# Attention heads on ScalarE: the exponential of a head issued ahead of the copy of the head before it

## What is computed

```
def attend_block(args):                      # a block of 128 query rows
    qb, iqb, iwb, start = args
    tpos = start + jnp.arange(QBLK)
    idx = indexer_topk(iqb, iwb, ik, tpos, k_sel)
    return sparse_attend(qb, k[bi, idx], v[bi, idx], idx, tpos, rel_bias)

def sparse_attend(q, kg, vg, idx, tpos, rel_bias):
    ...
    logits = jnp.einsum('bqhd,bqkhd->bqhk', q, kg).astype(jnp.float32) * (DH_A ** -0.5) + bias
    logits = jnp.where((dist >= 0)[:, :, None, :], logits, -jnp.inf)
    p = jax.nn.softmax(logits, axis=-1).astype(vg.dtype)
    return jnp.einsum('bqhk,bqkhd->bqhd', p, vg)
```

## Time and profile before

| what | value |
|---|---|
| median of 3 executions | 3505.79 us |
| lowest and highest | 3501.47 and 3506.33 us |
| the profiled execution | 3506.33 us |
| its span in the profile | 3504.8 us |
| PE busy in the span | 3318.3 us, 95% |
| DVE, ACT, POOL busy | 1562.3, 1138.2, 1204.6 us |
| mean granted TensorE clock | 0.966 of full speed |

### The profile page before, as it was taken

One profiled execution on the slowest core, in us unless ns is written; L12 is line 12 of the kernel. 1 busy time (PEld: TensorE's weight loads), 2 busy tenths in 40 slices (PEclk: granted clock), 3 DMA queues, 4 the chain that ended last, 5 costly groups with the idle time before them and its releaser, 6 DMA issues. The chain is left out here.

```text
span 3504.8 us, 57096 instructions
## 1 busy us (share of the span) xinstructions
PE 3318.3 (95%) x20476; PEld 3101.8 (89%) x20476; DVE 1562.3 (45%) x2739; ACT 1138.2 (32%) x2092; POOL 1204.6 (34%) x881
## 2 busy tenths in 40 slices
PE   6979989989999999999999999999889999999998
PEld 5569973666999999999899998988789999999998
DVE  4699982542321212122457677667742222212122
ACT  3512212442241312122345545455532322222132
POOL 2206842220412221222445556565444321222122
PEclk8989989996999999999999999999899999999999
DMA  4217654221311111112223232212422111111111
GB/s 130 55 31 135 196 175 137 61 78 50 62 48 48 44 46 48 48 42 65 79 63 98 92 97 78 91 57 91 146 89 89 43 48 48 48 42 48 48 43 72
DMA packets 344005, 263.87 MB, mean 75 GB/s; under 512 B 52134, under 2 KB 308150, under 8 KB 341910
## 3 DMA queue, kind: packets, MB, share of 16 engines
q1 hardware_dynamic: 322726, 232.16, 22.5%
q0 software_dynamic: 8192, 19.13, 1.6%
q10 hardware_dynamic: 12976, 11.11, 1.5%
HBM read 219.43 MB, written 44.76 MB: 75 GB/s over the span
## 5 line engine op out<-in xcount | busy, mean ns | idle before, releaser
L234 POOL TENSOR_TENSOR w_low_sb<-w_loaded_sb,w_high_sb 128x1024 fp32r<-128x1024 f32 (+1 forms) x278 | 570.0, 2057 | 1554.1 <-ACT w_high_sb L226 1536.2
L252 PE MATMUL psum<-act_high_sb,w_high_sb 128*128 128x344 f32 (+1 forms) x2400 | 769.9, 321 | 16.9 <-PEq L2713 10.5
L252 PE MATMUL psum<-act_low_sb,w_high_sb 128*128 128x344 f32 (+1 forms) x2400 | 768.1, 320 | 0.0
L252 PE MATMUL psum<-act_high_sb,w_low_sb 128*128 128x344 f32 (+1 forms) x2400 | 768.0, 320 | 0.0
L252 PE MATMUL psum<-second_high_sb,w_high_sb 128*128 128x344 f32 x1728 | 553.3, 320 | 0.5 <-PEq L2305 0.5
L252 PE MATMUL psum<-second_low_sb,w_high_sb 128*128 128x344 f32 x1728 | 551.9, 319 | 0.0
L252 PE MATMUL psum<-second_high_sb,w_low_sb 128*128 128x344 f32 x1728 | 551.9, 319 | 0.0
L252 PEld LDWEIGHTS psum<-act_high_sb,w_high_sb 128*128 128x128 f32 (+1 forms) x2400 | 451.0, 188 | 17.8 <-issue 16.6
L252 PEld LDWEIGHTS psum<-act_high_sb,w_low_sb 128*128 128x128 f32 (+1 forms) x2400 | 451.3, 188 | 0.4
L252 PEld LDWEIGHTS psum<-act_low_sb,w_high_sb 128*128 128x128 f32 (+1 forms) x2400 | 451.1, 188 | 0.4
L226 ACT CAST w_high_sb<-w_loaded_sb 128x1024 fp32r<-128x1024 f32 (+1 forms) x230 | 239.6, 1043 | 522.1 <-PE psum L252 498.0
(11 more groups left out here) (439 smaller groups left out, 4913.3 us busy)
## 6 DMA issues: line engine op xcount, KB each, us to landing
w_loaded_sb<-in_w_up SPq DMA_DIRECT2D x64, 512.0 KB, 4.1
w_loaded_sb<-in_w_down SPq DMA_DIRECT2D x64, 512.0 KB, 4.2
w_loaded_sb<-in_w_in_odd SPq DMA_DIRECT2D x48, 512.0 KB, 4.0
key_pages_sb<-in_cache_k SPq DMA_DIRECT2D x64, 256.0 KB, 2.8
ecay_sum_spread_sb<-decay_sum_scratch SPq DMA_DIRECT2D x8, 2048.0 KB, 9.8
w_loaded_sb<-in_w_in_even SPq DMA_DIRECT2D x28, 512.0 KB, 4.1
gated_scratch<-gated_sb POOLq DMA_DIRECT2D x8, 1032.0 KB, 4.4
ample_ssm_state_sb<-in_state_ssm SPq DMA_DIRECT2D x64, 128.0 KB, 6.9
```

The lines of the kernel that those rows point to most:

```text
L234: ins = self.nc.gpsimd.tensor_tensor(self.wl[:, par, k, 0:width], self.wf[:, par, k, 0:width], self.wh[:, par, k, 0:width].bitcast(F32), A ...
L252: ins = nc.tensor.matmul(out, w[:, par, k, 0:width], a[:, k, cols], start=n == 0, stop=n == 3 * KT - 1)
```

## The change

ACT's loop over the steps is reordered: in step n the exponential of n is issued first and the copy of the transposed probabilities of n - 1 after it. Before, the copy came first. The waits of each instruction stay with it; every other engine's stream is as it was. The last copy, of step 63, stays behind the loop.

```
             for n in range(N):
                 i, h = seq[n]
                 L = width(i)
-                if n >= 1:
-                    copy_turned(n - 1)
                 act.wait_ge(s_max, n + 1)
                 if h == 0 and i >= 2:
                     act.wait_ge(s_rden, i - 1)
                 nc.scalar.activation(logit[:, n % 2, 0:L], logit[:, n % 2, 0:L], ACT.Exp, bias=nm[:, n % 2:n % 2 + 1],
                                      accum_out=total[:, i % 2, h:h + 1]).then_inc(s_prob, 1)
+                if n >= 1:
+                    copy_turned(n - 1)
                 smp.values_act(act, n)
                 if n >= HA and n % HA == 2:
                     high(n // HA - 1)
```

## The result

The change makes the kernel slower: 3523.88 us as the median of five executions (3521.19 to 3528.72) against 3504.42 for five of before (3501.47 to 3506.33). The ratio is 1.0055 with a 95% interval of 1.0043 to 1.0068. The direction is the forecast one. The size is not: 19.5 us where 9.6 were worked out, and outside the range, whose upper end was 3523. The profiled execution took 3522.86 us. It lies 16.5 us above the profiled execution of before, so 3.0 of the 19.5 us are outside what the two traces can explain.

What follows compares the result with a forecast made beforehand. PE was taken to bound the kernel, busy 95% of the span, so only its gaps count. Terms 3.56 + 3.12 + 1.64 + 1.40 + 0.37 - 0.51 = +9.6 us on 3505.8 gave 3515.4 us, range 3510 to 3523.

Steps and rivals of the forecast that it cites:

- heads 0 to 30: Attention heads where PE's work on the samples' value pages hides the longer chain: cost nothing, upper end +1 us in all.
- head 31: Head whose max waits for VectorE's work on the samples' last values: its transposes come +0.37 us later.
- The odd intervals: Intervals between two heads' transposes that hold score products: no PE gap, to stay at 4.68 us in the last block.
- block 7: Last eight heads: even heads 56, 58, 60, 62 each +0.89 us as the copy waits behind the exponential, 3.56 us.
- block 6: Eight heads before the last block: four even heads at +0.78 us each, 3.12 us.
- block 5: Sixth block of eight heads, max late from VectorE's rotary work: four even heads at 0.41 us, 1.64 us.
- block 4: Fifth block of eight heads: two even heads at the full clock (36, 38) at +0.70 us, 1.40 us.
- last head: Head 63, whose transposes waited for its exponential: that wait goes, -0.51 us.
- Two lags of the chain: Within an even head's chain: copy 0.03 us after the exponential's accumulator, transposes 0.05 us after the copy.
- the clock as a rival: Longer PE idle from block 7's even intervals brings one to three half-clock falls, 3518 to 3530 us; chance 13%.
- all of it PE idle: Profile sign: the 101.4 us stretch, T(35) to the end of weighting, grows by about 9 us, only in PE idle.
- new stretches at clock 0.50: Sign named as showing the prediction wrong: half-clock stretches in the profile that were not there before.

Runs made afterwards that it cites:

- e5: The kernel before with the exponential ahead of the copy in heads 0 to 31 only: 3503.04 us against 3501.00, ratio 1.0006.
- e1: The changed kernel plus eight unused identity transposes on PE ahead of each even head's transposes from 34 on: 3512.64 us against 3503.49 for before, ratio 1.0029.
- e7: The kernel before plus four unused identity transposes on PE ahead of each even head's transposes from 34 on: 3505.25 us against 3501.00, ratio 1.0009.
- e10: The kernel before, each odd head's copy from 35 on done twice, plus eight unused transposes per even head from 34 on: 3512.73 us, ratio 1.0032 to before.
- e8: The changed kernel plus four unused identity transposes on PE ahead of each even head's transposes from 34 on: 3510.75 us against 3501.00 for before, ratio 1.0029.
- e3: The kernel before with the exponential ahead of the copy at even heads only: 3522.95 us, ratio 1.0059 to before.
- e9: The kernel before, its order kept, with the copy of each odd head from 35 on done twice: 3533.92 us against 3501.70, ratio 1.0090.
- e4: The changed kernel with products of heads n+2 and n+3 issued behind the transposes of even n: 3511.13 us against 3503.49 for before, ratio 1.0021.
- e11: As e4, but only from head 36 on; heads 42, 44, 50, 52, 58 keep the old places of products and copy: 3497.86 us against 3501.70, ratio 0.9992.

## Why the prediction was half of it

**Right: what bounds the stage, and which heads pay.** The even heads of blocks 4 to 7 carry the cost, heads 0 to 30 none (0.00 us from head 3 to head 30, in the changed kernel and in e5), head 31 +0.32 us against +0.37, and the next stage takes the shift one for one. The odd intervals stay at PE's own work.

**Right, a little too large: the terms of the order.** From e1, where the clock stays up: block 7 3.27 us (3.56 predicted), block 6 2.83 (3.12), block 5 1.84 (1.64), block 4 1.33 (1.40), last head -0.70 (-0.51). With -0.4 spread over the odd intervals that is the 8.2 us measured, against 3.56 + 3.12 + 1.64 + 1.40 - 0.51 = 9.2. Of the 1.0 us between them, 0.45 lie in the even heads, 0.36 in the odd intervals, which were put at nothing, and 0.19 in the last head. Two lags of the chain were wrong and nearly cancel, which is luck: I let the copy start 0.03 us after the exponential's accumulator had been read, and it starts 0.09 us before that ends (767.08 against 766.98 + 0.19 = 767.17); and I let T(62) start 0.05 us after the copy, where it starts 0.14 after (767.08 + 0.99 = 768.07 to 768.21). Block 5 is luck too. Its term of 0.41 a head was the middle between two arguments, and the heads 40, 42, 44 and 46 measure 0.67, 0.13, 0.33 and 0.71: the full term at two of them and little at the others.

**Wrong: the clock as a rival instead of a term.** The prediction worked out the idle time of 1.40 us in 4.22, saw that PE's busy share there would be lower than in the stretch ahead of the fall at 645.4, and still gave it 13 in 100 with the argument that the gaps so far had been harmless. The step that failed is "Against it: the gaps are split over work that kept the full clock up to now with 0.5 to 0.9 us of idle": a row about small gaps was used for gaps about twice as large, and the sum held nothing for the clock. What the runs show, as the waits of PE ahead of the transposes of the even heads 36 to 62 and the time at half clock in the stretch:

| kernel | waits, us | at half clock, us |
|---|---|---|
| before | 0.07 to 0.92 | 0 |
| e7, before with filler | 0 to 0.47 | 0 |
| e10, doubled copies with filler | 0 to 0.68 | 0 |
| e1, changed with filler | 0 to 0.71 | 0 |
| e8, changed with half the filler | 0.38 to 1.15 | 0 |
| changed | 0.49 to 1.59 | 20.5 |
| e3, exponential first at even heads | 0.06 to 1.59 | 29.1 |
| e9, doubled copies | 0.91 to 1.56 | 37.5 |

In the changed kernel the four falls come 0.4 to 1.6 us after the start of the transposes of heads 36, 40, 52 and 56, which had waited 1.23, 1.56, 1.26 and 1.59 us. The length of one wait doesn't settle it alone, though. The fall at 645.4 in the kernel before, outside this stretch, came behind a wait of 0.69 us:

```profile
644.56 0.74 PE L1844 MATMUL psum<-ident_sb,qkv_sb 128*128 128x128 f32 x5 [0.69 <-DVE sample_att_sb L1542]
```

And e4 had three waits of 1.10 to 1.34 us and no fall in the stretch. What is shown is that longer waits at every second head brought the falls, whatever made the waits, and that filling them took the falls away.

The missing term is 8.8 us in the profiled execution. The forecast that the added time would be "all of it PE idle" failed with it, and the sign that it had named itself, new stretches at clock 0.50, came true. The rival's price per microsecond was in the right place, 8.8 / 20.5 = 0.43 us lost for each at half clock, where "at most" half was allowed. The falls were more but shorter than it assumed, four of 3.4 or 6.8 us and not one to three of 10.2, and its 3518 to 3530 holds the measured time (the lower end by its own price should have been 3515.4 + 5.1 = 3520.5). The rule of the Trainium skill that was set beside this rival (TensorE: Matmul & The Clock Gate, "A second HAM failure mode: psum-queue depth-cycling") turned out to describe it; after the change the trace agrees, with four falls in 113 us, while before the change, with waits of up to 0.92 us at the same places, it did not.

The range followed from the same step: with that rival at its real weight it would have reached to 3530, and the terms as measured give 3504.4 + 8.2 + 0.3 + 8.8 = 3521.7. The median is 2.2 us above that; no run shows where these lie.

**Open:** why four of the fourteen gaps were followed by a fall and the others, such as 1.48 us at head 48, not, and why e3, with nearly the same gaps, has 29 us at half clock and the changed kernel 20.5. The five executions of the changed kernel spread over 7.5 us, and the slowest has the lowest mean clock (0.961, against 0.964 in the fastest). That need not come from the falls in this stretch: 22 executions of the kernel before, beside e1, spread over 9.3 us (3499.39 to 3508.67). Also open is how much of the 5.5 us that e11 gains in its stage reaches the end.

## What to carry to other kernels

Before moving an instruction ahead of one that is seen waiting, look in the timeline at when its own input arrives, at each kind of step: here the exponential's maximum came 0.7 us after the copy could have started (749.07 against 748.33), and the 122 us of waiting on ScalarE said nothing about that. A reorder on one engine can need its partner on another: exponential first loses 8 us of the stretch with the products where they were and gains 5, at the heads where it pays, with them one interval earlier. And where a change lengthens PE's idle gaps, cost the clock as a term and not as a remote rival; a few cheap dummy transposes in the gaps test for it in one run. That the clock held over gaps of one size said nothing here about gaps twice as long.

## What the runs showed of the hardware that was not expected

Work whose result nobody uses made a kernel faster: 120 extra transposes, 9 to 11 us (e1 against the changed kernel), and 21 us in e10 against e9. In e8 half as many did as well. The clock's falls cost more than the waits that brought them: in e9 17.7 us against 10.4. And the length of one idle gap did not tell whether the clock would fall: 0.69 us was followed by a fall (before, at 645.4), 1.34 us was not (e4, head 58).
